# Attention stage of a hybrid diffusion block: the first upper-half transfers of keys and queries on ScalarE's queue

## What is computed

```python
def windowed_attention(q, k, v, k_ctx, v_ctx, sink):
    # q [b,L,16,64], k/v [b,L,4,64], k_ctx/v_ctx [b,256,4,64], sink [16]
    def block(i):                        # 128 queries; keys of 3 blocks around them
        s_loc = einsum("bqkrd,bskd->bkrqs", qb, kb)       # masked to |i-j| <= 128
        s_ctx = einsum("bqkrd,bskd->bkrqs", qb, k_ctx)    # all 256 context keys
        p = softmax(concatenate([s_loc, s_ctx, s_sink], -1))
        return einsum(p_local, vb) + einsum(p_context, v_ctx)
```

## Time and profile before

| | |
|---|---|
| median of 3 runs | 2930.75 us (2930.63 to 2934.76) |
| profiled execution, its own time | 2933.16 us |
| its span, first to last instruction | 2931.5 us |
| mean granted TensorE clock | 0.915 |
| TensorE busy (PE) | 2504.5 us, 85% |
| VectorE (DVE) | 1597.0 us, 54% |
| ScalarE (ACT) | 1061.7 us, 36% |
| GpSimd (POOL) | 705.8 us, 24% |
| attention stage | from about 1312.6 us to about 1681 us of the span |

### The profile page before, as it was taken

The page is one execution under the profiler, slowest core; times in us unless marked ns, Lnnn a source line. Parts: engine busy times, 40 slices in busy tenths (PEclk is TensorE's granted clock), DMA queues, the critical chain, the costliest instruction groups (busy, mean ns, idle before and its releaser), DMA issues. The chain is left out here.

```text
span 2931.5 us, 31293 instructions
## 1 busy us (share of the span) xinstructions
PE 2504.5 (85%) x11848; PEld 1972.9 (67%) x11848; DVE 1597.0 (54%) x1674; ACT 1061.7 (36%) x1349; POOL 705.8 (24%) x487
## 2 busy tenths in 40 slices
PE   6799999999898996975989659698885499999992
PEld 2588888778697885653656448576474388888881
DVE  4455554431143665763556352532254699999994
ACT  3333333121131113541334341310232377777772
POOL 0001000010002434994992000000042212222113
PEclk8799999999999998996999869899697699999996
DMA  4333333342225867949564255543333599999994
GB/s 188 97 109 116 117 117 108 115 144 86 89 88 197 299 241 247 308 164 202 148 157 88 54 167 150 161 118 94 119 115 113 222 375 397 391 395 398 398 362 143
DMA packets 307553, 556.80 MB, mean 190 GB/s; under 512 B 22121, under 2 KB 212025, under 8 KB 283953
## 3 DMA queue, kind: packets, MB, share of 16 engines
q1 hardware_dynamic: 277938, 431.61, 43.3%
q0 software_dynamic: 27200, 115.10, 12.1%
q10 hardware_dynamic: 2304, 8.62, 0.8%
HBM read 434.22 MB, written 120.79 MB: 189 GB/s over the span
## 5 line engine op out<-in xcount | busy, mean ns | idle before, releaser
L2412 DVE TENSOR_TENSOR e_wlo<-e_w,e_whi 128x2048 fp32r<-128x2048 f32 x188 | 425.7, 2290 | 43.5 <-ACT e_whi L2365 42.2
L2365 ACT CAST e_whi<-e_w 128x2048 fp32r<-128x2048 f32 x192 | 366.3, 1915 | 120.8 <-PE e_gu L2525 83.5
L386 PE MATMUL f_lat<-h_hi,w_hi 128*128 128x512 f32 x800 | 254.4, 399 | 0.3 <-DVE w_lo L522 0.3
L386 PE MATMUL f_lat<-h_lo,w_hi 128*128 128x512 f32 x800 | 250.7, 394 | 0.0
L386 PE MATMUL f_lat<-h_hi,w_lo 128*128 128x512 f32 x800 | 250.6, 394 | 0.0
L522 DVE TENSOR_TENSOR w_lo<-w_raw,w_hi 128x1024 fp32r<-128x1024 f32 x50 | 61.3, 1225 | 216.9 <-ACT w_hi L447 216.9
L1889 PE MATMUL b_acc<-b_hi,b_whi 128*128 128x512 f32 x384 | 151.4, 394 | 14.0 <-DVE b_lo L1840 14.0
L1579 DVE CUSTOM_DVE_ANT_0 a_masked<-a_a_ps,a_mask 128x640 f32<-128x640 f32 x128 | 105.5, 825 | 99.3 <-PE a_a_ps L1483 95.9
L1510 PE MATMUL a_c_ps<-a_prob,a_v 128*128 128x512 f32 x304 | 157.8, 602 | 0.0
L386 PEld LDWEIGHTS f_lat<-h_hi,w_hi 128*128 128x128 f32 x800 | 136.0, 188 | 30.5 <-issue 4.8
L386 PEld LDWEIGHTS f_lat<-h_hi,w_lo 128*128 128x128 f32 x800 | 136.0, 188 | 27.7
(11 more groups left out here) (346 smaller groups left out, 5627.8 us busy)
## 6 DMA issues: line engine op xcount, KB each, us to landing
e_w<-in_w_gate_up SPq DMA_DIRECT2D x128, 1024.0 KB, 10.4
e_w<-in_w_down SPq DMA_DIRECT2D x64, 1024.0 KB, 8.7
w_raw<-in_w_in SPq DMA_DIRECT2D x50, 512.0 KB, 4.0
t_space<-xbcT POOLq DMA_DIRECT2D x18, 1280.0 KB, 6.4
before<-t_space SPq DMA_DIRECT2D x16, 1024.0 KB, 4.2
y_before<-before SPq DMA_DIRECT2D x64, 256.0 KB, 6.1
a_ada_w<-in_w_ada POOLq DMA_DIRECT2D x32, 512.0 KB, 4.1
b_w<-in_w_ssd_br SPq DMA_DIRECT2D x16, 1024.0 KB, 5.6
```

Of the source, the lines that this page charges most:

```text
L386: mm = nc.tensor.matmul(o, weights[:, b, k, :], part[:, k, a:a + n], start=(k == 0 and n_pass == 0), stop=(k == KT - 1 and n_pass == 2))
L2365: nc.scalar.copy(whi[:, slot % SPLIT], w[:, slot]).then_inc(w_hi, 1)
L2412: V.tensor_tensor(wlo[:, slot % SPLIT], w[:, slot], whi[:, slot % SPLIT].bitcast(F32), ALU.subtract).then_inc(w_split, 1)
```

## The change

SyncE's `load_k` no longer issues the transfer to `k1` high, and `load_q` issues the one to `q1` high only for tiles from 3 on. ScalarE issues these five transfers (near keys, query tile 0, far keys, query tiles 1 and 2) at the very start of its stream, before its first wait. Sources, targets, sizes and semaphores are the same.

```diff
--- before.py
+++ after.py
@@ -1372,28 +1372,31 @@
 
         with nc.Block() as block:
 
+            kH = qkH[QH * HD:, :].rearrange("(g d) t -> d g t", d=HD)
+            kL = qkL[QH * HD:, :].rearrange("(g d) t -> d g t", d=HD)
+            qH = qkH[0:QH * HD, :].rearrange("(h d) t -> d h t", d=HD)
+            qL = qkL[0:QH * HD, :].rearrange("(h d) t -> d h t", d=HD)
+            low, high = slice(0, HD), slice(HD, P)
+
+            def q_cols(m):
+                return slice(KV_LAT0 + m * P, KV_LAT0 + m * P + P)
+
             @block.sync
             def _(sp):
-                kH = qkH[QH * HD:, :].rearrange("(g d) t -> d g t", d=HD)
-                kL = qkL[QH * HD:, :].rearrange("(g d) t -> d g t", d=HD)
-                qH = qkH[0:QH * HD, :].rearrange("(h d) t -> d h t", d=HD)
-                qL = qkL[0:QH * HD, :].rearrange("(h d) t -> d h t", d=HD)
-                low, high = slice(0, HD), slice(HD, P)
-
                 def load_k(cols_, sem):
                     sp.dma_start(k1[low, :, cols_].bitcast(F32), kH[:, :, cols_]).then_inc(sem, 16)
-                    sp.dma_start(k1[high, :, cols_].bitcast(F32), kH[:, :, cols_]).then_inc(sem, 16)
                     sp.dma_start(k2[low, :, cols_].bitcast(F32), kL[:, :, cols_]).then_inc(sem, 16)
 
                 def load_q(m):
-                    j, at = m % QB, slice(KV_LAT0 + m * P, KV_LAT0 + m * P + P)
+                    j, at = m % QB, q_cols(m)
                     if m >= QB:
                         sp.wait_ge(b_made, FIRST[m - QB + 1])
                         sp.sem_inc(sp_carrier, 1)
                         for row in (TOP_HI, TOP_LO):
                             sp.dma_start(q2[row:row + 1, j].bitcast(F32), s.masks[1:2, 0:QH // 2, 0:CTX]).then_inc(q_in[j], 16)
                     sp.dma_start(q1[low, j].bitcast(F32), qH[:, :, at]).then_inc(q_in[j], 16)
-                    sp.dma_start(q1[high, j].bitcast(F32), qL[:, :, at]).then_inc(q_in[j], 16)
+                    if m >= QB:
+                        sp.dma_start(q1[high, j].bitcast(F32), qL[:, :, at]).then_inc(q_in[j], 16)
                     sp.dma_start(q2[low, j].bitcast(F32), qH[:, :, at]).then_inc(q_in[j], 16)
 
                 def load_top(m):
@@ -1555,6 +1558,12 @@
                         act.wait_ge(cols_out, 16 * n - 16)
                     nc.scalar.copy(cols[:, n % 2, PER_KV * g:PER_KV * g + PER_KV], c_ps[:, group % 2]).then_inc(kept, 1)
 
+                near, far = slice(0, KEYS), slice(KEYS, KV_TOK)
+                act.dma_start(k1[high, :, near].bitcast(F32), kH[:, :, near]).then_inc(near_in, 16)
+                act.dma_start(q1[high, 0].bitcast(F32), qL[:, :, q_cols(0)]).then_inc(q_in[0], 16)
+                act.dma_start(k1[high, :, far].bitcast(F32), kH[:, :, far]).then_inc(far_in, 16)
+                for m in range(1, QB):
+                    act.dma_start(q1[high, m].bitcast(F32), qL[:, :, q_cols(m)]).then_inc(q_in[m], 16)
                 act.wait_ge(v_in, 16)
                 act.wait_ge(v_ones, 1)
                 nc.scalar.copy(columns(v, 0, HD), vraw).then_inc(v_laid, 1)
```

## The result

The changed kernel takes 2916.47 us (median of 4 runs, 2911.77 to 2916.97), the kernel before in the same comparison 2932.76 us (4 runs): ratio 0.9939, 95% interval 0.9922 to 0.9956. It is faster by some 16 us. The forecast was 2920.8 us and a range down to 2917.0 us, so the result lies under the range. The saving is 16.3 us by this comparison (14.3 us against the 2930.75 us that the forecast started from), where 10.0 us were expected.

What follows compares the result with a forecast made beforehand. The prediction took the drain of SyncE's load queue to bound attention's start. Removed 14.6 us plus 10.9 us, less 15.5 us for 5.51 MB at 356 GB/s, saved 10.0 us: 2930.75 to 2920.8 us, range 2917.0 to 2932.5.

Steps and rivals of the forecast that it cites:

- I take an earlier start one for one: Attention stage: any earlier start of the matmul part shortens the whole time equally, the rest of the stage unchanged.
- main case: Attention's loading: halves run side by side at 281 to 417 GB/s, saving 5.9 to 12.3 us, 10.0 expected; chance 0.52.
- the same distance from there to the stage's end: Expected sign in the profile after: from the first column score to attention's end, time stays unchanged.
- The small term left at zero: Loading drain: perhaps one of GpSimd's 512 KB loads falls out of it, a gain of 1.3 us, not counted.
- The price of the change proper: Attention's loading: moving five upper-half transfers to ScalarE's queue makes the drain 10.0 us shorter.
- R: Joint rate of both queues over 5.51 MB mixed in attention's loading: bounds 216 to 417 GB/s, 356 taken.
- the halves run side by side: Attention's loading: lower-half and upper-half transfers from two queues proceed together, 356 GB/s expected against 216 for one half.
- The slack of the compute chain: Before the column scores: first tops ready near 1353.2 us, issued at 1356.7 us, so the drain stays the bound.
- The turns packet for packet, which the prediction had by bytes: SyncE's and ScalarE's queues in the loading: turns about equal by bytes, so ScalarE moves about SyncE's 2.36 MB.
- Rival A: Attention's loading: engines take turns and hardly gain, 200 to 280 GB/s, 2930.8 or 2929.3 us; chance 0.41.
- Rival B: Slower: ScalarE's transfers come ahead of what is needed and mixing costs throughput, 3.8 us lost at 188 GB/s; chance 0.07.

Runs made afterwards that it cites:

- e8: Changed kernel with GpSimd's w_ada loads begun 6.3 us earlier, behind 14 memsets instead of the wait for far keys; 2928.19 us, ratio 0.9980 to before.
- e2: Kernel before with GpSimd's w_ada loads cut to 16 of 1024 columns (modulation not the reference's); 2910.53 us, ratio 0.9922 to before.
- e3: Changed kernel with GpSimd's w_ada loads cut to 16 of 1024 columns (modulation not the reference's); 2909.52 us, ratio 0.9920 to before.
- e4: Kernel before with five memsets on GpSimd, so its w_ada loads begin 9.0 us later; 2919.89 us, ratio 0.9959 to before.
- e9: Kernel before with GpSimd's w_ada loads waiting for the first tops' transfers instead of the far keys; 2922.67 us, ratio 0.9962 to before.
- e10: Changed kernel with GpSimd's w_ada loads waiting for the first tops' transfers instead of the far keys; 2916.41 us, ratio 0.9944 to before.
- e5: Changed kernel with extra loads ahead, 2.49 MB to the lower half by SyncE, the same to the upper by ScalarE; 19.5 us to the first ordinary issue.
- e15: Changed kernel with ScalarE waiting for the constants before issuing its last three transfers; 2922.79 us, ratio 0.9961 to before.
- e14: Changed kernel with three memsets on GpSimd, so its w_ada loads begin 5.5 us later; 2917.37 us, ratio 0.9943 to before.
- e11: Changed kernel with SyncE spreading a block's inverse before loading the query tile after next; 2939.70 us, ratio 1.0022 to before.

## Why the prediction was wrong

**The step that failed** is "I take an earlier start one for one". The start came 8.6 us earlier, inside the main case's 5.9 to 12.3, but the loop behind it, put at no change, became 9.3 us shorter as well; "the same distance from there to the stage's end" was the sign that failed. The loop does not wait only on what belongs to it: GpSimd's stream of 512 KB loads for a later stage runs through it, tied to the far keys and not to the loop. e8 shows that moving this stream back to its old place takes the loop's gain away with ScalarE's queue unchanged; e2 and e3 show that without its bytes the two kernels have loops of 285.8 and 288.1 us and times 1.0 us apart. A higher clock is part of the gain but not a cause of its own: its fall at 1480 us follows a stall and makes it dearer.

**The small term left at zero** was large. The loads of w_ada in the drain were put at 1.3 us. By e2, e4 and e9 the kernel before has a start of 56.6 to 57.6 us without them, not 64.9: 7 to 8 us. In the changed kernel they still cost 2.9 us (e3). What takes the rest out is, by the order of issues, that the tops are issued 8.9 us earlier while the far keys, on which GpSimd waits, are in at the same time as before (43.6 and 43.3 us). I had expected the far keys earlier too.

**The price of the change proper was oversized**: 10.0 us were expected, 3.4 (e3 against e2) and 2.8 (e10 against e9) were measured at the column scores, and 5.2 and 4.9 at the issue of the tops. In whole times the same pairs give 1.0 and 6.3 us. Two errors made that:
- R. The mechanism was right, the halves run side by side. But rates near the 356 GB/s assumed, 346 in e5 and 332 in one window here, were seen only late in the loading, in e5 with runs of 512 bytes against each other; with keys in the mix it was 238 to 258. The 4.92 MB that both queues moved up to 1333 us took about 17.5 us (the first tile's 20.8 us less some 3.3 us ahead of the first data and behind the last, an estimate), or 281 GB/s, where 13.3 us were predicted. This put the first tile 1.3 us later, not 3.1 us earlier, and the constants, as far behind it as predicted (5.1 us against 5.3), at 25.8 us, not 21.8.
- The slack of the compute chain. The chain of the 16 row scores behind the constants, predicted to be ready 3.5 us before SyncE wants the tops, now gives ScalarE's part of them at 44.2 us, right where the queue would let them go (45.1 us). Without the loads of w_ada it is the row scores of the second tile, and no longer the drain, that the column scores wait for (e10). The turns packet for packet, which the prediction had by bytes, matter little here: ScalarE's queue had moved 2.57 MB where 2.36 were predicted.

That the start came out near the forecast (8.6 against 10.0) is luck, two errors that cancel: the halves give 3.4 us of it, the loads the other 5.

**The rivals.** Rival A, with the Trainium skill's rule behind it (page "SBUF — State Buffer", "Can I just issue two DMAs to hit both halves?": 6% more, they serialise), is refuted here: 26.7 us against 19.5 for the same bytes. Its number, less than 5.9 us saved, is nearer to what the change proper brings (5.2 us of drain, 3.4 us of start) than the main case's 10.0, but for another reason than a lack of gain from the two halves. Rival B's mechanism, constants delayed by transfers that are not yet needed, was real (3.1 us later, and e15 gives back 5.7), but it only ate part of the gain.

**Not settled:** why a given run's loop collides more or less. Times of one kernel differ by up to 15 us (e4, e14), and the profiles tie the loop to the waits for the inverse only in groups. The steps from the store of the inverse to its spreading narrow it down. For the first three blocks they take 3.7, 7.7 and 5.2 us before and 4.8, 5.6 and 3.4 in e8. With query tiles but small w_ada loads they take 2.4, 1.5 and 1.5 (e2) and 2.9, 1.8 and 1.5 (e3), and with w_ada but no query tile ahead 3.9, 1.5 and 1.5 (e11). So the steps over 4 us were seen only where both were there. But in e11 a spreading took 8.5 us to land beside a w_ada load, so whether GpSimd's packets hold the inverse up directly, or through query tiles that they delay, is not separated.

## What to carry to other kernels

Loads to 64 partitions ran at 203 to 220 GB/s here, where loads to 128 had 356; a second queue that wrote the other half at the same time was worth 1.2 to 1.7 times that by the windows (26.7 us down to 19.5 for the probe's bytes), one that wrote the same half was worth nothing. What such a queue gains has to be followed to the next bound, and transfers that are not needed first should not be issued beside those that are. Above all, before an earlier start is booked one for one, look for a stream on another engine that is not tied to the same event: shifting the two against each other moved the time of the changed kernel by 11.7 us (e8), more than the 1.0 to 6.3 us of the change itself, and a small test (shrink that stream's bytes) shows it at once.

## What the runs showed of the hardware that was not expected

- Two queues of SyncE and ScalarE alternate packet for packet: 662 to 662, 603 to 609, 1006 to 998, 690 to 693 in four windows, with packets from 512 bytes to 3.5 KB.
- One half from each queue: 248 GB/s with 3.5 KB packets, 305 to 346 with nearly all packets of 512 bytes; both queues to the lower half: 203 to 209 in every window from 1318 to 1338 us.
- An 8 KB store that takes 1.5 us from its issue to the next one took 7.7 us behind a query tile and beside w_ada loads.
- A TensorE wait in this loop goes with more than its own length: 1.7 us of loop for each us, over 16 profiles.
